# A hybrid RWKV and latent-attention layer: gate projections of the second branch moved into the RWKV passes

## What is computed

```python
xn = rmsnorm(x, g_mix)
proj = xn @ w_in                        # 2048 x 9728
p_a, p_b, p_g = split(proj)             # RWKV 3520 | MLA 2112 | gates 2 x 2048
y_a = rwkv7_mix(p_a, ...) @ w_o_a       # 16 heads of 64: token shift, decay, delta state
q, c_kv, k_r = split(p_b)               # 8 heads of 128 + 64, latent of 512
o = attend(q, latent, rope key)         # prompt: chunk-causal; sample: 128 past rows + new
y_b = o @ w_o_b
gate_a, gate_b = split(sigmoid(p_g))
h = x + (gate_a * y_a + gate_b * y_b) @ w_out
h = h + (silu(conv(hn @ w_gate)) * (hn @ w_up)) @ w_ffn_down     # hn = rmsnorm(h)
```

## Time and profile before

| | us |
|---|---|
| median of 3 runs | 2792.08 |
| the runs | 2786.61 to 2792.92 |
| span of the profiled execution, first to last instruction | 2783.1 |
| mean granted clock of TensorE | 0.978 |
| a pass, of eight | about 94 |
| mix | 203 |

### The profile page before, as it was taken

The page is one execution under the profiler, slowest core; times in us unless marked ns, Lnnn a source line. Parts: engine busy times, 40 slices in busy tenths (PEclk is TensorE's granted clock), DMA queues, the critical chain, the costliest instruction groups (busy, mean ns, idle before and its releaser), DMA issues.

```text
span 2783.1 us, 41528 instructions
## 1 busy us (share of the span) xinstructions
PE 2644.5 (95%) x15596; PEld 2425.2 (87%) x15596; DVE 1224.6 (44%) x1928; ACT 926.5 (33%) x1310; POOL 184.3 (7%) x222
## 2 busy tenths in 40 slices
PE   6999999999998999999999979999999999999997
PEld 6878877877887888998998769999987899999885
DVE  4555564555554333332443344444433344444333
ACT  4332333233223333443332233333322233333222
POOL 3011211120110100000000000000000000000010
PEclk9999999999999999998999999999999999999998
DMA  5212111211123322332444324444433344444433
GB/s 161 85 56 60 55 43 56 60 49 49 49 58 97 95 90 76 103 94 85 126 128 164 123 83 128 125 124 128 128 121 125 124 128 124 124 128 128 141 124 120
DMA packets 414049, 283.21 MB, mean 102 GB/s; under 512 B 31680, under 2 KB 392642, under 8 KB 412720
## 3 DMA queue, kind: packets, MB, share of 16 engines
q1 hardware_dynamic: 405168, 259.16, 30.7%
q0 software_dynamic: 8832, 23.36, 2.7%
HBM read 275.55 MB, written 6.92 MB: 101 GB/s over the span
## 4 chain that ended last, share of the span: by engine, by line
PE 87%; DVE 6%; ACT 4%; issue 2%; DMA 1%; DVEq 0%; ACTq 0%; POOL 0%; SPq 0%; POOLq 0%
PE banks L1259 18%; PE banks L731 16%; PE banks L733 15%; PE banks L732 15%; PE banks L409 2%; PE banks L419 2%; PE banks L742 2%; PE banks L744 2%; PE banks L743 2%; PE banks L417 2%; PE banks L314 1%; PE banks L1157 1%; PE banks L426 1%; PE banks L1149 1%; DVE t_y L628 1%
## 5 line engine op out<-in xcount | busy, mean ns | idle before, releaser
L721 DVE TENSOR_TENSOR w_lo<-w_raw,w_hi 128x1024 fp32r<-128x1024 f32 x482 | 590.2, 1225 | 970.9 <-ACT w_hi L716 967.5
L731 PE MATMUL banks<-x_hi,w_hi 128*128 128x384 f32 x2640 | 923.6, 350 | 9.4 <-DVE w_lo L721 6.5
L733 PE MATMUL banks<-x_hi,w_lo 128*128 128x384 f32 x2640 | 892.0, 338 | 0.0
L732 PE MATMUL banks<-x_lo,w_hi 128*128 128x384 f32 x2640 | 891.7, 338 | 0.0
L716 ACT ACTIVATE w_hi<-w_raw 128x1024 fp32r<-128x1024 f32 x482 | 510.8, 1060 | 914.5 <-PE banks L733 527.5
L731 PEld LDWEIGHTS banks<-x_hi,w_hi 128*128 128x128 f32 x2640 | 502.9, 190 | 24.1 <-issue 9.7
L732 PEld LDWEIGHTS banks<-x_lo,w_hi 128*128 128x128 f32 x2640 | 503.1, 191 | 5.1 <-issue 2.1
L733 PEld LDWEIGHTS banks<-x_hi,w_lo 128*128 128x128 f32 x2640 | 501.8, 190 | 0.0
L1259 PE MATMUL banks<-w_hi,act_hi 128*128 128x512 f32 x528 | 164.1, 392 | 4.6 <-DVE h_rows L1746 2.4
L1259 PE MATMUL banks<-w_lo,act_hi 128*128 128x512 f32 x528 | 164.0, 392 | 0.0
L1259 PE MATMUL banks<-w_hi,act_lo 128*128 128x512 f32 x528 | 163.6, 391 | 0.0
(11 more groups left out here) (400 smaller groups left out, 2987.1 us busy)
## 6 DMA issues: line engine op xcount, KB each, us to landing
w_raw<-in_w_ffn_in SPq DMA_DIRECT2D x176, 512.0 KB, 3.7
w_raw<-in_w_in SPq DMA_DIRECT2D x144, 512.0 KB, 3.8
w_raw<-in_w_ffn_down SPq DMA_DIRECT2D x88, 512.0 KB, 3.6
w_raw<-in_w_out SPq DMA_DIRECT2D x32, 512.0 KB, 3.6
w_raw<-in_w_o_a SPq DMA_DIRECT2D x16, 512.0 KB, 3.8
w_raw<-in_w_o_b SPq DMA_DIRECT2D x16, 512.0 KB, 3.8
w_raw<-in_w_in SPq DMA_DIRECT2D x20, 256.0 KB, 3.8
w_ukv_head<-in_w_ukv POOLq DMA_DIRECT2D x8, 512.0 KB, 5.1
```

Source lines behind the costliest of these rows:

```text
L721: nc.vector.tensor_tensor(lo[:, s], raw[:, s], hi[:, s].bitcast(F32), ALU.subtract).then_inc(lo_done, 1)
L731: nc.tensor.matmul(out, hi[:, s, k, :], xh[:, kt, :], start=kt == 0, stop=False)
L732: nc.tensor.matmul(out, hi[:, s, k, :], xl[:, kt, :], start=False, stop=False)
L733: last = nc.tensor.matmul(out, lo[:, s, k, :], xh[:, kt, :], start=False, stop=kt == 15)
```

## The change

- The 16 gate tiles of the second branch are projected in the RWKV passes, two in each: a pass (the last too) now has 6 tiles, 48 pieces and cuts 0 to 11. The third and fourth of a pass are gate tiles. ScalarE copies each raw to one buffer (`gst`), POOL stores it to HBM (196 KB) and tells that the buffer is free.
- In `pe_rwkv` the added pieces go before the sum of squares (5 for 1), before the token transposes (5 for 4), before and after the triangular products, one to each level, and to the end. The cuts move along: cut 3 now stands before the levels, and level lv has cut 4 + lv on ScalarE and VectorE.
- The mix reads the raw gates back in two halves of 8 tiles (1.57 MB each), asked for after the sample values. ScalarE makes the sigmoid of two tiles in one instruction. A pair is now one tile of w_o_b; the outputs go through four banks in turn.
- Sample values: the weights of all 8 heads are loaded ahead, after the last prompt head, and 32 products go to two banks without a wait between; the results are split straight from the banks instead of being copied to `mla_out` first.
- VectorE and ScalarE split the attention output in parts of four heads, the prompt part first.
- A few semaphores are merged.

```diff
@@ pe_rwkv @@
             last.then_inc(E("lora_ps"), 1)
-            pieces(1)
+            pieces(5)
             pe.wait_ge(E("kk_sq_done"), f + 1)
...
             last.then_inc(E("s0_ps"), 1)
-            pieces(4)
+            pieces(5)
...
             last.then_inc(E("as_ps"), 1)
-            pieces(1)
+            pieces(2)
...
             last.then_inc(E("mt_ps"), 1)
-            pieces(1)
+            pieces(2)
...
                 last.then_inc(E("dt_ps"), 1)
-                pieces((2, 2, 2, 1, 1)[lv])
+                pieces((3, 3, 3, 2, 2)[lv])
@@ act_rwkv @@
             fn(gg[:, :], ps[:, 5, 0:NT], ACT.Copy).then_inc(E("gates_done"), 1)
+            cut(1)
...
             fn(s0t[:, :, :], ps[:, 7, :].rearrange("p (b v) -> p b v", b=NB), ACT.Copy).then_inc(E("s0_done"), 1)
-            cut(1)
+            cut(2)
...
             fn(asd[:, :], ps[:, 5, 0:P], ACT.Copy).then_inc(E("as_done"), 1)
-            cut(2)
+            cut(3)
...
                     .then_inc(E("g_done"), 1)
-                if lv != 3:
-                    cut((3, 4, 5, 0, 6)[lv])
+                cut(4 + lv)
+            cut(9)
@@ dve_rwkv @@
             for lv in range(5):
-                if lv in (0, 1, 3):
-                    cut((3, 4, 0, 5)[lv])
+                cut(4 + lv)
                 dve.wait_ge(E("dt_ps"), f * 5 + (lv + 1))
@@ POOL, in each pass @@
+                for g in range(2):
+                    j = 2 * f + g if last else f * 2 + g
+                    pool.wait_ge(proj_taken, f * PER_FT + (T_IT + 4 + g))
+                    pool.dma_start(gate_b_kept[j] if last else gate_b_kept[bass.ds(j, 1)].squeeze(0), gst[:, :])\
+                        .then_inc(sem("gate_b_out"), 16)
+                    pool.wait_ge(sem("gate_b_out"), f * 32 + 16 * (g + 1))
+                    pool.sem_inc(sem("gate_b_stored"), 1)
@@ POOL, after the sample attention @@
+            pool.wait_ge(sem("ohd_ps"), 2)
+            pool.wait_ge(stores, 32)
+            for half, gb in enumerate((gb_lo, gb_hi)):
+                pool.dma_start(gb[:, :, :], gate_b_kept[8 * half:8 * half + 8].rearrange("j p n -> p j n"))\
+                    .then_inc(sem(f"gate_b_in{half}"), 16)
@@ TensorE, sample values and mix @@
+            pe.wait_ge(E("w_uv_in"), 16 * FT)
+            for e in range(FT):
+                w = wuv[:, e] if e < FT - 1 else wuv_last
+                for kc in range(4):
+                    last = mm_(unit(6, e), w[:, kc, :], qld[:, kc, e, :], start=kc == 0, stop=kc == 3)
+                if e % 4 == 3:
+                    last.then_inc(E("ohd_ps"), 1)
...
-            with pe.Fori(0, KD // 2) as i:
-                for q in range(2):
-                    pe.wait_ge(proj_taken, i * 2 + (T_MIX + KD + q - 1))
-                    for s in range(2):
-                        pe_block(i * 3 + (T_MIX_B + q), s, ps[:, q, 0:NT])
-                pe.wait_ge(E("ob_split"), FT)
-                for s in range(2):
-                    pe.wait_ge(E("b_taken"), OPEN + i * 2)
-                    pe_half(i * 3 + (T_MIX_B + 2), s, obh, obl, ps[:, 2 + s, 0:NT])
+            pe.wait_ge(E("ob_split"), 4)
+            with pe.Fori(0, KD // 4) as i:
+                for pr in range(2):
                     for s in range(2):
+                        pe.wait_ge(E("b_taken"), i * 4 + (2 * pr + s + 1))
+                        pe_half(i * 2 + (T_MIX_B + pr), s, obh, obl, ps[:, 2 * pr + s, 0:NT])
@@ ScalarE, mix @@
+            def mix_gates(half, i):
+                g = (gb_lo, gb_hi)[half][:, bass.ds(i * 2, 2), :]
+                fn(g, g, ACT.Sigmoid).then_inc(proj_taken, 1)
+
+            def mix_pair(n, last):
+                t = n + T_MIX_B
                 for q in range(2):
                     if not (last and q == 1):
+                        act_hi(t + 1, q, t * 16 + 112)
+                    act.wait_ge(E("mixed"), n * 2 + (q + 1))
...
                     fn(dst, mm[:, q, :], ACT.Copy).then_inc(E("mix_hi"), 1)
```

More of the change, by code:

```diff
@@ L671, in dve_rwkv @@
                 if c == 0:
-                    cut(7)
+                    cut(10)
                 if c < 2:
@@ L825, in _ @@
                 tile_in(T_LORA + j, lambda s: w_in[s][:, :, c:c + P])
-            with sp.Fori(0, FT) as f:
-                for q, (c, w) in enumerate(((0, P), (W, P), (2 * W, P), (Q0, 192))):
-                    tile_in(T_FT + q + f * 4, lambda s: w_in[s][:, :, bass.ds(f * w + c, P)])
-            for j in range(9):
-                t = T_MLA + j
+            HEAD_COLS = ((0, P), (W, P), (2 * W, P), (Q0, 192))
+            gate_b = lambda j: G0 + D + j * P
+            for q, (c, w) in enumerate(HEAD_COLS):
+                tile_in(T_FT + q, lambda s: w_in[s][:, :, c:c + P])
@@ new lines, in _ @@
+            with sp.Fori(0, FT - 1) as f:
+                for q in range(PER_FT):
+                    if q in (3, 4):
+                        cols = f * (2 * P) + gate_b(q - 3)
+                    else:
+                        c, w = HEAD_COLS[min(q, 3)]
+                        cols = f * w + (c + w)
+                    tile_in(f * PER_FT + (T_IT + q), lambda s: w_in[s][:, :, bass.ds(cols, P)])
+            for q in range(PER_FT):
+                c = gate_b(2 * (FT - 1) + q - 3) if q in (3, 4) else CKV0 + min(q, 3) * P
+                tile_in(T_CKV + q, lambda s: w_in[s][:, :, c:c + P])
@@ L843, in _ @@
-            for t0, g, w, j0, pairs in ((T_MIX, 0, 0, KD // 2, 4), (T_MIX + 12, 0, 0, 0, 4), (T_MIX_B, D, 1, 0, 8)):
-                with sp.Fori(1, pairs + 1) as i1:
+                    g0 = Q0 + 384 * j
+                    for g, c in enumerate((g0 + 128, g0 + 320) if j < 4 else (KR0, KR0)):
+                        block_in(t, s, raw[:, s, :, 64 * g:64 * g + 64], w_in[s][:, :, c:c + 64])
+            for t0, j0 in ((T_MIX, KD // 2), (T_MIX + 12, 0)):
+                with sp.Fori(1, 5) as i1:
@@ L1478, in mix_pair @@
[L1478 to L1486 removed]
+            act.wait_ge(E("old_ps"), NB)
@@ L1492, in mix_pair @@
                     fn(dst, mm[:, q, :], ACT.Copy).then_inc(E("mix_hi"), 1)
-            with ch.loop(KD // 2 - 1, 0) as i:
-                mix_pair(i, False)
+            for half in range(2):
+                act.wait_ge(E(f"gate_b_in{half}"), 16)
+                with ch.loop(4 - half, 0) as i:
+                    mix_gates(half, i)
+                    mix_pair(i + 4 * half, False)
+            mix_gates(1, 3)
             mix_pair(KD // 2 - 1, True)
@@ new lines, in _, with mix_pair, residue @@
+            for h in range(2):
+                dve.wait_ge(E("obh_done"), h + 3)
+                tt(obl[:, 4 * h:4 * h + 4, NP_:NT], ps[:, 6 + h, :].rearrange("p (e t) -> p e t", e=4),
+                   obh[:, 4 * h:4 * h + 4, NP_:NT].bitcast(F32), S).then_inc(E("ob_split"), 1)
+            dve_lo(T_MIX_B, 1)
+            def mix_pair(half, i, pr, last):
+                n = i * 2 + pr
+                t = n + (T_MIX_B + 4 * half)
+                tile_of = lambda x, j: x[:, j, :] if last else x[:, bass.ds(j, 1), :].squeeze(1)
+                def residue(q):
+                    j = n * 2 + (8 * half + q)
@@ L1732, in mix_pair @@
                     dve.wait_ge(E("mix_hi"), j + 1)
                     tt(tile_of(ml, j), mm[:, q, :], tile_of(mh, j).bitcast(F32), S).then_inc(E("mix_done"), 1)
-            with ch.loop(KD // 2 - 1, 0) as i:
-                mix_pair(i, False)
-            mix_pair(KD // 2 - 1, True)
+                for q in range(2):
+                    j = n * 2 + (8 * half + q)
+                    if not (last and pr == 1 and q == 1):
+                        dve_lo(t + 1, q)
+                    if q == 1:
+                        residue(0)
+                    dve.wait_ge(proj_taken, n + (4 * half + T_MIX + KD + 1))
+                    dve.wait_ge(blk_used, t * 2 + (1 + q))
+                    tt(mm[:, q, :], ps[:, 2 * pr + q, 0:NT], tile_of((gb_lo, gb_hi)[half], n * 2 + q), M)\
+                        .then_inc(E("b_taken"), 1)
+                    dve.wait_ge(E("b_taken"), j + (OPEN + 4))
+                    tt(mm[:, q, :], mm[:, q, :], tile_of(ga, j), A).then_inc(E("mixed"), 1)
@@ L1739, in add_acc @@
+                residue(1)
+            with ch.loop(2, 0) as i:
+                for pr in range(2):
+                    mix_pair(0, i, pr, False)
+            with ch.loop(1, 0) as i:
+                for pr in range(2):
+                    mix_pair(1, i, pr, False)
+            mix_pair(1, 1, 0, True)
+            mix_pair(1, 1, 1, True)
             def add_acc(c, need, done):
```

229 lines of the change are left out of this document (100 added, 129 removed).

## The result

| | before | changed |
|---|---|---|
| median, us | 2789.35 | 2892.84 |
| the runs (4 each) | 2783.05 to 2792.92 | 2885.30 to 2896.06 |
| ratio, with its 95% interval | | 1.0372 (1.0356 to 1.0388) |
| span of the profiled execution, us | 2783.1 | 2891.0 |
| mean of passes two to seven, us | 94.01 | 124.08 |

The kernel became 3.7% slower; 5% was forecast. The span grew by 107.9 us. 237.7 of it lie ahead of the first sample value, where 133.2 us of matmuls came in, so 104.5 us are waits and clock. Behind it the span is 129.8 us shorter, with 133.2 taken out, so the stretch from the first sample value on costs 3.4 more than the moved work alone explains. (The 133.2 us are the prediction's price of 16 tiles.)

What follows compares the result with a forecast made beforehand. With TensorE busy in 95% of the span, only its work and its waits could move the time. Passes +68 (added waits less filled ones), clock +67 and mix +7 made +142 us, so 2934 us, range 2850 to 2990.

Steps and rivals of the forecast that it cites:

- The added wait: In the five levels of each pass, pieces wait for blocks split in the same level: 15.4 us a pass, +14.5 net.
- The waits filled: In each pass, added pieces cover TensorE's waits, most at the square (line 362, -4.0): -6.0 us, between nothing and -7.5.
- The clock: In the passes, four new waits each bring half clock, 2.2 us lost each, less 0.4: 8.4 a pass, +67 us.
- The mix: From the first sample value on, ScalarE and VectorE's chain bounds a pair at 9.7 us: -125.9 against -133.2, +7 us.
- A price: On TensorE, a matmul of 384 columns costs 0.1735 us at full clock; 16 moved tiles make 133.2 us.
- The time around the span: Whole kernel: the median of the runs lies 9.0 us above the trace's span, so 2925 and 9 give 2934 us.
- Rival 1: In the passes, the waits come but the clock stays: 2867 us, chance 0.10.
- Rival 3: In the levels of the passes, the lower clock sticks, about 25 us a pass: 3067 us, chance 0.05.
- Rival 2: In the passes, the splits stay ahead of the levels and the kernel gets faster: 2743 us, chance 0.09.

Runs made afterwards that it cites:

- e1_lead: The change with block 5 split before the first level and each later block one level earlier on ScalarE and VectorE; 2732.55 us.
- e2_behind: The change with the piece between a level's first matmuls and the next product moved behind the level's matmuls, cuts untouched; 2776.12 us.
- e3_twice: The change with ScalarE making the high part twice in cuts 4 to 8, so each split comes later by one copy; 2953.36 us.
- e5_values: The kernel before with only the sample values part: all value weights loaded at once, outputs split from the PSUM banks; 2777.03 us.
- e8_fill: Against e1_lead with a later mix sigmoid and one moved piece (2720.05 us): one piece moved before the bonus sum, one ahead of the mean; 2739.40 us.
- e9_swap: The change with ScalarE's split ahead of the gate tile's taking in cuts 4, 6 and 8; 2878.77 us.
- e7_sigmoid: The change with the mix's sigmoid of a pair of tiles moved behind ScalarE's first split of the pair; 2893.68 us.

## Why the prediction was right in kind and too high by 41 us

**The added wait: right.** The place (cuts 4 to 8, the piece between lines 418 and 426), the chain and its size were as forecast: 14.4 us a pass where 15.4 were worked out, 115.6 against 123 in all. Each of the five listed waits came out 0.2 us under its number (3.54 for 3.7, 2.89 for 3.1). The chain itself was exact: the low part ends 5.07 us behind the level's first matmuls (265.06), and the 0.2 is between counting the wait from the pace of the matmuls and counting it from their length. e1_lead, e2_behind and e3_twice show it from three sides: split earlier, and it goes; nothing behind it, and it costs little; split later by 1.1 us, and each wait grows by 1.1.

**The waits filled: right in sum.** Up to the first sample value e1_lead, with the new pieces and no late split, needs 77.8 us more than before for 133.2 us of work, a gain of 55.4. I had 6.0 and 0.9 a pass, 55, and 3 from the clock. But its make-up was another: the waits that the list of TensorE shows in the passes fell from 49.9 to 20.2 us, only 3.7 a pass; and half-clock time fell from 41.0 to 3.4 us, up to 2.3 a pass, where I had credited 0.4.

**The clock: this is the step that failed.** "The change has four waits of 3.1 to 3.7 us in each pass", each followed by "2.2 us" of loss, less 0.4 for the old stretch: 8.4 us a pass, +67. Three things were off. The stretches are 27, 3.4 a pass and not 4. None is 6.83 us long, so one costs 1.6 us at the rows' pace and 1.7 at 0.50, not 2.2: at most 5.8 us a pass instead of 8.8 (e1_lead shows 44.3 / 8 = 5.5). And the old clock loss that went was larger than 0.4: 41.0 us at half clock are 2.6 a pass at 0.50. Net, half-clock time in the passes rose by 51.2 us, which is 26 us at 0.50, where 67 stood in the sum. I took the mean of the two stretches in the earlier trace rows, one in each of two passes, for all; the shorter one was the better guide. The Trainium skill (TensorE: Matmul & The Clock Gate, HAM oscillation) has the cost come back with each round of waits, and the 27 stretches agree. By the same page's under 1% (What's actually happening) the term would have been under 28 us, an estimate. The gross loss of 40 to 46 us is 1.4 to 1.6% of the span; only the net one, 26, lies under that figure.

**The sum.** The old clock loss stands in the waits filled and in the net clock figure, so only one of the two may be used. With the gross figure: waits added 115.6 us (123 forecast), waits filled with the old clock loss -55.4 (-58), new clock loss 44.3 (70), from the first sample value on 3.4 (7), together 107.9 against 142. The new clock loss has 26 of the 34 us between them. The 44.3 is a remainder, so the four must add up; that it is mostly clock rests on the pace at half clock, not on the sum. Had it been taken net, the waits filled would be 3.7 us a pass and not 6.9, and the two errors would partly cancel.

**The mix: right, +3.4 for +7.** e5_values puts a gain of 8.1 us in it for the sample values, so the mix behind them lost some 11, where 8 and 15 were forecast. The products took 9.1 us to the first mix matmul (1515.93 to 1525.05), 9 were forecast. The first half of the gates landed after 8.2 us, not 10.7; a pair took 9.2 us, not 9.7. The second half took 12.2 us, hidden by the first four pairs.

**A price.** The prediction takes 0.1735 us for a matmul of 384 columns from 1151 in 200.5 us. That quotient is 0.1742; 0.1735 is the pace of the starts in a dense stretch (0.17 and 0.18 by turns). For the 16 tiles it makes 0.5 us.

**The time around the span.** I added 9.0 us to the new span, the difference between one profiled execution and the median of three other runs. The changed kernel's profiled execution took 2892.91 us with a span of 2891.0, so 1.9 lie around it. The rest of the 9.0 was scatter between runs. Against the span the forecast is 34 us too high (142 for 107.9), with this 41 against the median.

**The rivals.** Rival 1 (waits, no clock cost, 2867) is 26 us off, so the clock counted, at well under what I gave it. Rival 3 fell: every stretch of the changed kernel's passes is 3.41 us long, so between two waits the clock came back. Rival 2 described e1_lead before there was one: splits ahead, 2743 forecast, 2732.55 measured.

## What to carry to other kernels

- When work is dealt in small pieces into the gaps of a dependent chain, count which piece opens the next block, and compare that with where the block is made ready. A piece moved one place too early costs more than the wait that it fills, since an engine's queue is in order and the chain stands behind it. Twice here (the change, e8_fill) a move of this kind cost more than it filled.
- Adding pieces ahead of a stage shifts the need for every later block. The preparation on the other engines must move by as many places; here a few lines on two engines were worth 160 us.
- Price the clock by counting the stretches in the trace and taking their commonest length, 0.44 to 0.46 us for each us at half clock that is filled with matmuls, and take the old kernel's own loss off, once.

## What was not expected of the hardware

- In these kernels the time at half clock grows with the length of the recurring waits. In the passes of e2_behind, with 56 waits of 0.7 to 0.9 us and 6 of 1.2 to 1.3, there was no stretch at half clock. With one wait of 2.3 us in six of the passes, e8_fill had 6 stretches, 27.3 us; with one of 3.5 in six, the kernel before had 9, 41.0 us. With four a pass it was 22 stretches, 75.1 us, for waits of 2.9 to 3.3 (e9_swap), 27 with 92.2 us for 2.9 to 3.6 (the change), and 35 with 150.2 us for 4.0 to 4.6 (e3_twice).
- Two loads of 1.5 MB on one queue, issued together, landed after 8.2 and 12.2 us; beside them a load of the output weights came late, and ScalarE waited 2.4 us for it in e7_sigmoid, 0.7 in the change.
